# A two-layer hybrid block in fp32: order of the first attention's TensorE queue, and how its head norms are summed

## The reference, cut to what matters

```
def diff_attention(q1, q2, k1, k2, v, lam, ...):     # 8 heads, head dim 64 (two maps), value dim 128
    def probs(qb, k):
        s = einsum('bqhd,bkhd->bhqk', qb, k) * scale
        return softmax(where(mask, s, -inf))           # mask: chunk-causal, chunks of 64, meta tokens first
    a = probs(qb1, k1) - lam * probs(qb2, k2)
    return einsum('bhqk,bkhd->bqhd', a, v)
...
o = diff_attention(...)
o = rms_norm(o, g_sub) * (1.0 - lam_init)              # over the 128 values of a head
h = h + o.reshape(B, L, H * 128) @ w_o
```

## Time and profile before

| | |
|---|---|
| median of three runs | 2028.56 us |
| profiled execution: its own time | 2028.63 us |
| its span | 2026.8 us |
| first attention, heads 1 to 7 | about 60 to 250 us of the span |
| second attention | about 718 to 866 us |

### The profile page before, as it was taken

The page is one execution under the profiler, slowest core; times in us unless marked ns, Lnnn a source line. Parts: engine busy times, 40 slices in busy tenths (PEclk is TensorE's granted clock), DMA queues, the critical chain, the costliest instruction groups (busy, mean ns, idle before and its releaser), DMA issues.

```text
span 2026.8 us, 37421 instructions
## 1 busy us (share of the span) xinstructions
PE 2009.0 (99%) x13376; PEld 1804.8 (89%) x13376; DVE 1317.6 (65%) x2199; ACT 852.0 (42%) x1499; POOL 1164.9 (57%) x1395
## 2 busy tenths in 40 slices
PE   9999999999999999999999999999999999999998
PEld 9999899999999988899999998777788888988987
DVE  7777757857746868757857778865512457857654
ACT  5444434433423577634433425344422234433433
POOL 6445356675757522146675767744455557766765
PEclk9999999999999999999999999999999999999999
DMA  5222122232233311122232323322223223232322
GB/s 190 84 74 72 53 85 92 84 117 92 92 97 115 94 34 42 32 89 94 67 131 94 104 94 105 104 84 83 74 93 103 84 84 95 83 125 83 125 83 84
DMA packets 51986, 183.06 MB, mean 90 GB/s; under 512 B 5648, under 2 KB 7824, under 8 KB 51856
## 3 DMA queue, kind: packets, MB, share of 16 engines
q1 hardware_dynamic: 50304, 178.87, 27.3%
q10 hardware_dynamic: 1552, 2.42, 0.4%
HBM read 179.17 MB, written 2.10 MB: 89 GB/s over the span
## 4 chain that ended last, share of the span: by engine, by line
PE 93%; DVE 4%; issue 1%; ACT 1%; POOL 1%; DMA 0%; DVEq 0%; ACTq 0%; SPq 0%
PE ps L805 25%; PE ps L806 24%; PE ps L807 24%; PE ps L929 3%; PE ps L930 3%; PE ps L931 3%; PE ps L1180 2%; PE ps L1197 1%; PE ps L1190 1%; PE ps L1090 1%; PE ps L1121 1%; POOL w_lo L759 1%; PE ps L1105 0%; PE ps L1191 0%; PE ps L1407 0%
## 5 line engine op out<-in xcount | busy, mean ns | idle before, releaser
L739 POOL TENSOR_TENSOR w_lo<-w_raw,w_hi 128x256 fp32r<-128x256 f32 x1140 | 964.1, 878 | 744.5 <-ACT w_hi L2256 735.9
L805 PE MATMUL ps<-x_hi,w_hi 128*128 128x264 f32 (+2 forms) x2504 | 823.0, 329 | 0.0
L806 PE MATMUL ps<-x_lo,w_hi 128*128 128x264 f32 (+2 forms) x2504 | 813.5, 325 | 0.0
L807 PE MATMUL ps<-x_hi,w_lo 128*128 128x264 f32 (+2 forms) x2504 | 812.3, 324 | 0.0
L805 PEld LDWEIGHTS ps<-x_hi,w_hi 128*128 128x128 f32 x2504 | 471.3, 188 | 49.6 <-issue 5.4
L806 PEld LDWEIGHTS ps<-x_lo,w_hi 128*128 128x128 f32 x2504 | 470.8, 188 | 42.1 <-issue 0.2
L807 PEld LDWEIGHTS ps<-x_hi,w_lo 128*128 128x128 f32 x2504 | 471.3, 188 | 39.6
L2256 ACT ACTIVATE w_hi<-w_raw 128x1024 fp32r<-128x1024 f32 x267 | 278.0, 1049 | 72.1 <-PE ps L807 56.4
L805 PE MATMUL ps<-g_hi,w_hi 128*128 128x264 f32 (+3 forms) x648 | 207.9, 321 | 1.0 <-DVE g_lo L1916 1.0
L806 PE MATMUL ps<-g_lo,w_hi 128*128 128x264 f32 (+3 forms) x648 | 205.9, 318 | 0.0
L807 PE MATMUL ps<-g_hi,w_lo 128*128 128x264 f32 (+3 forms) x648 | 205.6, 317 | 0.0
(11 more groups left out here) (278 smaller groups left out, 3044.1 us busy)
## 6 DMA issues: line engine op xcount, KB each, us to landing
w_raw<-stream SPq DMA_DIRECT2D x334, 512.0 KB, 3.5
h<-x_t SPq DMA_DIRECT2D x4, 528.0 KB, 6.7
out_t<-h SPq DMA_DIRECT2D x6, 256.0 KB, 2.3
scratch<-rotary_tables ACTq DMA_DIRECT2D x4, 264.0 KB, 5.4
out_t<-h ACTq DMA_DIRECT2D x2, 256.0 KB, 2.5
par<-params ACTq DMA_DIRECT2D x1, 342.0 KB, 4.7
scratch<-positions ACTq DMA_DIRECT2D x1, 256.0 KB, 2.6
cst<-shape_constants ACTq DMA_DIRECT2D x1, 193.0 KB, 6.2
```

Source lines behind the costliest of these rows:

```text
L739: last = nc.gpsimd.tensor_tensor(w_lo[:, ring(j), cols], w_raw[:, j % 4, cols], w_hi[:, ring(j), cols].bitcast(F32), ALU.subtract)
L805: nc.tensor.matmul(out_ap, w_hi[:, s, c], xh[:, k, cols], start=first, stop=False)
L806: nc.tensor.matmul(out_ap, w_hi[:, s, c], xl[:, k, cols], start=False, stop=False)
L807: return nc.tensor.matmul(out_ap, w_lo[:, s, c], xh[:, k, cols], start=False, stop=last)
```

## The change

Five edits go together.

1. At the seam of two heads with a norm sum, the order on TensorE becomes scores of units 1 to 4, value transposes, sum of squares. Where there is no sum yet (head 0) the value transposes stay first. ScalarE takes `exps(hd + 1, 1)` right after `take_values`, ahead of `sub_rms`.
2. The sum of squares of heads 0 to 5 is made from two fp32r parts (`sub_sum_of_parts`): ScalarE writes the high part after unit 3's weights, GpSimd the low part between two weight halves. GpSimd's loops are written out by head for that.
3. VectorE makes a unit's combination and takes a projection piece before a step of the norm.
4. In the last head the order is new on three engines: output-projection blocks come before the sum of head 6, whose sum goes to banks 2 and 5; 6 passes more of the second tile are done before the last head's factor is needed (`held=1`).
5. The second attention's meta scores use 128 stationary columns in place of 16.

```
+            def head_sum_low(n, par_):
+                pool.wait_ge(head_sum_hi, n + 1)
+                nc.gpsimd.tensor_tensor(sum_lo, sq[:, par_, :], sum_hi.bitcast(F32),
+                                        ALU.subtract).then_inc(head_sum_lo, 1)
+            def head_tiles(hd, par_, j, i=0):
+                for m in range(3):
+                    lo_part(j + m, i, stride=8)
+                head_sum_low(hd - 1, 1 - par_)
+                lo_part(j + 3, i, stride=8)
...
             def tile_pair(...):
...
-                        for b in range(blocks - 1 - m, blocks):
+                        for b in range(blocks - (held if m else 1), blocks):
...
             def scores_of_b(h, idx):
...
-                s = scores_b(idx)
+                s = scores_b(idx) if t else ps[:, 4, UNIT_COLS[2] + UNIT_COLS[3]:UNIT_COLS[2] + UNIT_COLS[3] + META]
...
-                    last = nc.tensor.matmul(s[:, k0:k1], q_b[rows, h % 4, q0:q0 + nq], k_b[rows, h % 4, k0:k1],
+                    last = nc.tensor.matmul(s[:, k0:k1], q_b[rows, h % 4, q0:q0 + P], k_b[rows, h % 4, k0:k1],
...
+            def sub_sum_of_parts(n, pieces):
+                pe.wait_ge(r_ready, N_SUB + n)
+                pe.wait_ge(head_sum_lo, n + 1)
+                for bank, t0, width in chunks(T1):
+                    pe.wait_ge(chunk_taken, pieces + bank)
+                    out_ap = ps[:, bank, 0:width]
+                    nc.tensor.matmul(out_ap, ones[:, :].bitcast(F32R), sum_hi[:, t0:t0 + width], start=True, stop=False)
+                    last = nc.tensor.matmul(out_ap, ones[:, :].bitcast(F32R), sum_lo[:, t0:t0 + width], start=False, stop=True)
+                last.then_inc(ss_ready, 1)
...
             def head_a(hd, par_, sums=True, before=True):                      # TensorE
-                for idx in range(1, 5):
-                    step(scores, idx)
                 for idx in range(5):
...
+                if not sums:
+                    value_transposes(hd + 1, 1 - par_)
+                for idx in range(1, 5):
+                    scores(hd + 1, 1 - par_, idx)
                 if sums:
-                    sub_sum(hd - 1, 1 - par_, 0, 6 * hd + 11)
-                value_transposes(hd + 1, 1 - par_)
+                    value_transposes(hd + 1, 1 - par_)
+                    sub_sum_of_parts(hd - 1, 6 * hd + 11)
             def last_head_a():                                                  # TensorE
                 hd, par_ = HEADS_A - 1, 1
-                for idx in range(1, 5):
-                    scores(hd, par_, idx)
                 transposes(hd, par_, 0)
-                sub_sum(HEADS_A - 2, 0)
+                pe.wait_ge(ln_done, N_SUB + HEADS_A - 2)
+                wo_blocks(0, 0, 0, 5)
                 values(hd, par_, 0)
+                pe.wait_ge(exp_done, 5 * hd + 2)
+                sub_sum(HEADS_A - 2, 0, (2, 5))
                 transposes(hd, par_, 1)
-                pe.wait_ge(ln_done, N_SUB + HEADS_A - 1)
-                wo_blocks(0, 0, 0, 5)
+                wo_blocks(0, 1, 0, 5)
                 values(hd, par_, 1)
                 transposes(hd, par_, 2)
-                wo_blocks(0, 1, 0, 5)
+                wo_blocks(0, 0, 5, 6), wo_blocks(0, 1, 5, 6)
                 values(hd, par_, 2)
                 transposes(hd, par_, 3)
-                wo_blocks(0, 0, 5, 6), wo_blocks(0, 1, 5, 6)
+                wo_blocks(0, 0, 6, 7), wo_blocks(0, 1, 6, 7)
                 values(hd, par_, 3)
                 transposes(hd, par_, 4)
-                wo_blocks(0, 0, 6, 7), wo_blocks(0, 1, 6, 7)
+                pe.wait_ge(ln_done, N_SUB + HEADS_A - 1)
+                wo_blocks(1, 0, 0, 2)
                 values(hd, par_, 4)
...
-                wo_blocks(1, 0, 0, 3)
-                sub_sum(HEADS_A - 1, 1, 4)
-                wo_blocks(1, 0, 3, 6), wo_blocks(1, 1, 0, 6)
+                wo_blocks(1, 0, 2, 6)
+                sub_sum(HEADS_A - 1, 1, (4, 5))
+                wo_blocks(1, 1, 0, 7), wo_blocks(1, 0, 6, 7)
...
             def head_a(hd, par_, norms=True):                                   # VectorE
                 for idx in range(4):
+                    combine(hd, par_, idx + 1)
+                    piece_a(hd + 1, 1 - par_, idx)
                     if norms and idx < 3:
                         (sub_scale, sub_hi, sub_lo)[idx](hd - 2)
-                    combine(hd, par_, idx + 1)
-                    piece_a(hd + 1, 1 - par_, idx)
                     take_output(hd, par_, idx)
...
             def last_head_a():                                                  # VectorE
+                combine(hd, par_, 1)
                 sub_scale(hd - 2)
-                combine(hd, par_, 1)
+                combine(hd, par_, 2)
+                sub_hi(hd - 2), sub_lo(hd - 2)
                 take_output(hd, par_, 0)
-                sub_hi(hd - 2), sub_lo(hd - 2)
-                combine(hd, par_, 2)
+                combine(hd, par_, 3)
+                sub_scale(hd - 1)
                 take_output(hd, par_, 1)
-                sub_scale(hd - 1)
-                combine(hd, par_, 3)
+                sub_hi(hd - 1), sub_lo(hd - 1)
+                combine(hd, par_, 4)
                 take_output(hd, par_, 2)
...
             def head_a(hd, par_, j, i=0):                                       # ScalarE
                 for idx in range(5):
+                    if idx in range(1, 4):
+                        exps(hd, par_, idx + 1)
+                    take_transposed(hd, par_, idx)
...
+                    if sums and idx == 3:
+                        act.wait_ge(sq_ready, SQ[N_SUB] + hd)
+                        A.activation(sum_hi, sq[:, 1 - par_, :], ACT.Copy).then_inc(head_sum_hi, 1)
                 take_values(hd + 1, 1 - par_)
+                exps(hd + 1, 1 - par_, 1)
                 if isinstance(hd, int) and hd == HEADS_A - 2:
                     sub_square(hd, par_)
                 if sums:
                     sub_rms(hd - 1)
             def last_head_a():                                                  # ScalarE
-                exps(hd, par_, 1)
                 take_transposed(hd, par_, 0)
-                sub_rms(hd - 1)
-                for idx in range(1, 4):
-                    exps(hd, par_, idx + 1)
-                    take_transposed(hd, par_, idx)
+                exps(hd, par_, 2)
+                sub_rms(hd - 1, (2, 5))
+                take_transposed(hd, par_, 1)
+                exps(hd, par_, 3)
+                take_transposed(hd, par_, 2)
+                exps(hd, par_, 4)
+                take_transposed(hd, par_, 3)
                 take_transposed(hd, par_, 4)
```

More of the change, by code:

```diff
@@ L516, in program @@
         u_copied = sem("u_copied")
+        head_sum_hi = sem("head_sum_hi")
+        head_sum_lo = sem("head_sum_lo")
         post_step = sem("post_step")
@@ L732, in _, with lo_part @@
         def _(pool):
-            def lo_part(j, i=0, ordered=True):
-                pool.wait_ge(hi_ready, j + 1 + 4 * i)
+            def lo_part(j, i=0, ordered=True, stride=4):
+                pool.wait_ge(hi_ready, j + 1 + stride * i)
                 if ordered:
-                    wait(pool, half_done, j - 3 + 4 * i)
+                    wait(pool, half_done, j - 3 + stride * i)
                 for c in range(0, HW, HW // LO_CUTS):
@@ L776, in _ @@
             first_lo_part()
-            for j in range(1, 4):
-                lo_part(j)
-            begun = 4
+            def head_sum_low(n, par_):
[7 more added lines that the diff above has]
+                lo_part(j + 3, i, stride=8)
+            for j in range(1, 11):
+                lo_part(j)
+            head_tiles(1, 1, 11)
+            with pool.Fori(0, (HEADS_A - 4) // 2) as i:
+                for n in range(2):
+                    head_tiles(2 * i + 2 + n, n, 15 + 4 * n, i)
+            head_tiles(HEADS_A - 2, 0, 31)
+            begun = 4 * (HEADS_A - 2) + 11
             for d in DOWNS.values():
@@ L831, in pair_blocks, with tile_pair @@
                            b == 0, False)
-            def tile_pair(j, tl, blocks, xh, xl, T, ready, begun=False):
+            def tile_pair(j, tl, blocks, xh, xl, T, ready, begun=False, held=2):
                 if not begun:
@@ L845, in tile_pair, with tiles @@
                     last.then_inc(half_done, 1)
-            def tiles(j, tl, n, blocks, xh, xl, T, ready, after_first=None, paired=False, begun=False, T_odd=None):
+            def tiles(j, tl, n, blocks, xh, xl, T, ready, after_first=None, paired=False, begun=False, T_odd=None, held=2):
                 done = 0
@@ L855, in tiles @@
                 if paired:
-                    tile_pair(j, tl, blocks, xh, xl, T, ready, begun)
+                    tile_pair(j, tl, blocks, xh, xl, T, ready, begun, held)
                     done = 2
@@ L872, in norm_sum @@
             def norm_sum(steps, T, src=acc, semaphore=acc_step, bank0=6, pieces=0):
```

(27 more changed lines are left out.)

3 lines of the change are left out of this document (removed).

## The result

The changed kernel takes 2042.73 us (median of six runs, 2041.37 to 2044.16) against 2028.5 for the one before: a ratio of 1.0068, 95% interval 1.0057 to 1.0078. It is slower by 14 us; I had forecast 2.7 faster, and the range ended at 2027.9. The profiled execution took 2044.16 with a span of 2042.3. One of the eleven executions of e1 took 9038.8 us, for a cause that nothing here shows, and its ratio leaves that one out.

The account below looks back on a forecast made before the run. The prediction took TensorE, busy 99% of the span, as the bound. Its terms, seams -2.6, last head +0.8 and meta scores -0.9, summed to -2.7, so 2025.9 us, with a range of 2023.2 to 2027.9 for 8 in 10.

Parts of the forecast that it names:

- Transposes and piece take 3.52: 6.99: Seam, TensorE: transposes 0 and a projection piece run from 3.47 to 6.99 us after the start of `values(hd, 4)`.
- that very wait: Last head: TensorE stalls 2.4 us after transposes 0, before the first output blocks, for Ln of head 5's sum.
- The term of the sum: Seams into heads 2 to 6: 8.32 us against 8.84, a gain of 0.52 each, 2.6 for five.
- the last head, forecast at +0.8: Last head in its new order: a loss of 0.8 us, bounds a gain of 0.6 and a loss of 1.8.
- The wait for the value copies: Seam: a new TensorE stall of 0.4 us before unit 0's transposes, for ScalarE's value copies.
- The wait before unit 1's transposes: Seam: TensorE's wait of about 0.6 us for VectorE's combination goes, as the reduction of unit 1 starts earlier.
- From the last sum to the last factor: Last head: 5.15 us from the last sum to the last factor's release, on ScalarE and VectorE alone, stays.
- The stall of the values of unit 2 in the last head: Last head: values of unit 2 wait for `take_output(1)`, behind unit 3's combination on VectorE; a stall of 0.6 us.
- a stall of 0.2 before unit 0's values: Seam: TensorE waits 0.2 us for ScalarE's copy of unit 0's transposes, ending at 7.15 behind Ln and Exp.
- The meta scores: Second attention: 0.10 us less for each of 16 products, lost in seven even heads; gain 0.9, bounds 0 and 1.6.
- The rival of the open load: Meta scores: 128-column loads cost their duration, 3.1 us in place of the 0.9 gain; total 2029.9, chance 0.04.
- The slower rival: Seam: ScalarE's longer queue delays the copy of unit 0's transposes by 1.64 us; +5.5, total 2034, chance 0.05.

Follow-up runs that it names:

- e1: Changed kernel with ScalarE taking the norm's Ln and Exp right after the value copies, ahead of unit 1's exponentials; 2024.75 us, ratio 0.9978 to the kernel before.
- e2: Changed kernel with useless fp32 products on TensorE between transposes 0 and the wait for Ln; 2038.9 us, ratio 1.0049 to the kernel before.
- e8: e1 with VectorE's norm steps ahead of the combinations again, in the heads but the last; 2025.09 us, ratio 0.9982 to the kernel before.
- e6: e1 with the last head's old order on TensorE, ScalarE and VectorE; 2025.81 us, ratio 0.9984 to the kernel before.
- e7: e1 with the value transposes and the sum in parts moved between unit 1's scores and those of units 2 to 4; 2022.4 us, ratio 0.9969.
- e3: Kernel before with only ScalarE's exponentials of unit 1 put ahead of the norm's Ln and Exp; 2051.01 us, ratio 1.0105.

## Why the prediction was wrong

**The step that failed** is "Transposes and piece take 3.52: 6.99". I let the projection piece behind transposes 0 start at once. It is written over banks 0 and 1, where the sum of squares lies until Ln has read it, and `piece_a` waits for `ln_done` for its first part. I had ScalarE's times right to 0.02 (Ln at 5.14, measured 5.12; the copy at 6.42, measured 6.40) and followed them to one consumer, the values, and not to the other. For the last head I had that very wait (2.4 forecast, 2.47 measured) and took it as something new there; in the five seams before it the same semaphore stands in a helper's argument. The term of the sum was -2.6 for five seams; measured, it is +12.5. From `values(1, 4)` to `values(6, 4)` it is 136.7 in e1, 146.2 in e2 and 152.1 in the changed kernel: -2.9 for the rest of the change, +9.4 for the wait, +6.0 for the clock. So the wait by its bare length was enough to turn the gain into a loss.

**A term that was missing** is the clock. I priced a wait at its length. Behind waits of 1.76 and more TensorE ran at 1.2 GHz for a while. That also spoils the last head, forecast at +0.8 and measured at +4.0: up to its last sum it took 23.7 instead of 20.5, and 2.6 of these 3.2 are clock by e2.

**Right in its mechanism.** The wait for the value copies: 0.4 forecast, 0.34 to 0.54 measured, six times. The wait before unit 1's transposes ended, and for the reason given: the combination was laid out for 7.8 after t0 and ended at 7.75 in e8. From the last sum to the last factor it was to stay at 5.15 and was 5.07 (262.72 to 267.79). The stall of the values of unit 2 in the last head: 0.6 forecast, 0.65 measured. Without Ln's delay the seam takes 8.44 (e1), where I had laid out 8.32. That they are so close is in part luck: the 8.32 holds a stall of 0.2 before unit 0's values, which no run has, and the 8.44 holds 0.25 before the piece. The last head without the wait for Ln is neither a loss nor a gain (e6).

**The meta scores** came out as written: 0.10 each, swallowed in the seven even heads, 0.9 in the sum, 0.9 to 1.0 in the traces. The rival of the open load is out by the same rows. The prediction says of the loads that their time scales with the columns and that the durations agree; with 92 and 189 ns for 16 and 128 columns they agree in direction only.

**The slower rival** put the bound in the right queue, ScalarE's at the seam, but with the wrong consumer, the copy of the transposes; that one was on time. Its price, 2034, was 9 us short.

**The sum again with what was measured**: +12.5 - 0.9 + 4.0 + 0.3 for the start of the run = 15.9, against 15.5 between the spans, the rest lying outside these landmarks. With the norm first (e1) the five seams give 136.72 - 139.63 = -2.9, the meta scores -0.9 and the last head -0.3, which is -4.1; the start of the run is 0.8 later, so -3.3, against -3.6 between the two profiled spans. The medians differ by 4.1.

## What to carry to other kernels

When an instruction moves back in one engine's queue, list every semaphore that it or anything behind it raises, and every queue that waits for each; look above all for the release of a buffer (here a PSUM bank) that a wait in another helper stands for, since such a wait is invisible in the profile before as long as it is met. Price a wait on a busy TensorE at its length and then ask what the granted clock does behind it: here 1.8 us of waiting cost 3.3. Where an engine waits for another's answer to a short piece of its own work, issue that piece earlier, between longer ones: in e7 the value transposes and the sum between the scores hid both waits.

## What the runs showed of the hardware

Some 2 us in the midst of dense work in which TensorE was busy for only 0.27 of 2.03 were enough to halve its granted clock, and the same time filled with useless products on half of the columns kept it at 1.00. A somewhat shorter wait did not do it: in the seam into head 6 of the changed kernel it was 1.46 and the clock stayed at 1.00,

```profile
213.70:215.90 2.20, 0.74 (x5) 0.53 (x5) 2.06 (x8) 1.87 (x6) 1.01 (x2) 1.00 0.01 4
215.90:219.00 3.10, 3.05 (x25) 3.08 (x26) 1.15 (x3) 3.10 (x7) 0.28 (x1) 1.00 0.50 167
```

while in the last head, after a wait of 2.47, the mean over 6.1 us was 0.53:

```profile
245.90:252.00 6.10, 6.07 (x27) 6.04 (x28) 3.94 (x10) 2.20 (x7) 0.00 (x0) 0.53 0.06 24
```

The seam into head 6 was 10.03 with the clock up, and 11.71 to 12.26 in the four others with the clock down, in one and the same execution. Its piece came 0.13 sooner than in the nearest of them (5.92 after t0 against 6.05), so about 1.5 of the difference is the clock: its cost can be read off a single trace. The seams of e3 show that this cost varies, 12.7 to 13.9 behind waits of the same 2.72.
